# A decoder layer on one core: group loop rotated, blocks written in token layout, values and decay exponents in single-pass matmuls

## The chip, the cores and the metric

The kernel runs on 1 core of one Trainium2 chip. The metric is device time in microseconds (us), the median of three runs. The core has a matrix engine (PE), a vector engine (DVE), a scalar engine (ACT), GpSimd (POOL) and a DMA issuer (SP). Each engine executes its own instructions in the order in which they are written, and waits on semaphores that the others raise. Matrix results land in eight PSUM banks; everything else lives in SBUF. The weights come from HBM by DMA.

## The reference, cut to what matters

The layer takes x of 512 tokens by 1024 channels, in float32. One normalised input feeds an attention branch (16 heads in 4 groups, compressed, selected and window attention) and a state-space branch (32 heads in 4 groups); a gated MLP follows. With 512 tokens and 8 blocks of 64, top-8 selects every block, so the selected branch is causal attention over its own keys and values.

```python
h = rms_norm(x, norm1_w)
(q, k_c, v_c, k_s, v_s, k_w, v_w, g_nsa, z, xbc, dt_raw, gate_a, gate_b) = split_columns(h @ w_in, IN_SIZES)
# attention: for each head, branches c (31 compressed keys), s and w (512 keys each)
p_c = masked_softmax(s_c - slopes * d_c, vis_c) * any_visible
p_s = masked_softmax(q @ k_s.T - slopes * d, causal)
p_w = masked_softmax(q @ k_w.T - slopes * d, causal)
o   = gate0 * (p_c @ v_c) + gate1 * (p_s @ v_s) + gate2 * (p_w @ v_w)
# state space, chunks of 128 tokens
xbc = silu(causal_depthwise_conv(xbc, conv_w, conv_b))      # width 4
decay_mat = exp(segsum(dt * a))                             # 128 x 128 for each head and chunk
y_diag = (C @ B.T * decay_mat) @ (x * dt)
y = y_diag + exp(a_cum) * (C @ state) + d_skip * x
y = rms_norm_per_group(y * silu(z)) * norm_w
merged = sigmoid(gate_a) * (y_a @ w_proj_a) + sigmoid(gate_b) * (y_b @ w_proj_b)
x = x + merged @ w_out
x = x + (silu(gate) * val) @ w_down                         # after rms_norm, w_up and a width-3 conv
```

## The kernel before, in words

**Weight blocks.** All projections are cut into 175 units of 1024 x 128 weights. SP loads a unit into `wraw` (2 buffers). ACT copies it, rounded to the short format fp32r, into `whi` (`hi`, L847), DVE subtracts to get the rest `wlo` (`lo`, L1233); 3 slots. PE then makes three matmuls of 512 columns for each of 8 slices (`ktile`, L477): whi x h_hi, whi x h_lo, wlo x h_hi. The 24 matmuls of a block accumulate in one of two banks g. Weights are stationary and tokens stream, so a block comes out with channels on partitions. An fp32r matmul is one pass; an fp32 matmul is shown as two passes in the trace.

**Phases.** A start phase (9 blocks), the loop over 4 groups (14 blocks each), 12 blocks of gates, the two projections and their merge, the output projection, the MLP. `between` in `gemm` (L485) names what PE does ahead of the k-th of the 8 slices of a block: in this way all small work of the group loop stands between slices.

**The group loop** (L580 for PE, L957 for ACT, L1330 for DVE). Blocks 0 to 3 are x, 4 and 5 are B and C, 6 to 9 are z, 10 to 13 are the next group's queries, keys and values, kept in `chan`.

- *Start.* `to_tokens` (L588) transposes the four blocks of `chan`, ACT copies them to `tok`, DVE squares, sums (L1373, L1375) and takes a Newton root, scales six heads into `tokn` (L1382); `backs` (L595) transposes these back; ACT makes a full copy (`full`, L1003) and a rounded copy (L1005) of each, DVE subtracts (`head_lo`, L1388). `comp_scores` (L601) makes the compressed scores in 32 small matmuls.
- *Eight attention units* n = 0 to 7 (4 heads, 2 branches). `scores(n)` (L619) writes the causal scores in fp32r; `ttr` (L1404) adds the bias `hbias`, negates and reduces; `exps` (L1024) takes four exponentials; `scale` (L1445) multiplies by 1/sum and gate; `p_transposes` (L650) transposes ten 128 x 128 tiles through the banks t0 and t1 in four fills j = 0 to 3; ACT copies each fill to `pT` (L1045), which releases the bank (`t_rel`), and the weighted values (L675) follow behind the block of the unit, in fp32, with 64 rows of output. `conv` (L1339) makes the depthwise convolution on DVE: one tensor_scalar and three scalar_tensor_tensor.
- *State space.* x and z are transposed to tokens (`xz_transposes`, L685); `am` (L1480) builds a masked exponent matrix, `seg` (L696) multiplies it by a triangle in four fp32 matmuls of 128 columns for half a chunk; ACT exponentiates (`seg_e`, L1073); DVE multiplies by C B^T (L1523); PE applies the result (L735). Eight steps k, with state updates, `combine` (L1505) and a last root (L1549). Then y is scaled, transposed (L749) and spilled to HBM, to be read back for the projections.

## Time and profile before

| | before |
|---|---|
| median of 3 runs | 1397.42 us (1395.48 to 1399.1) |
| profiled execution | 1396.07 us, span 1394.3 us |
| mean granted TensorE clock | 0.991 |
| PE busy | 1336.0 us (96%) |
| PE weight loads busy | 1052.5 us (75%) |
| DVE busy | 822.7 us (59%) |
| ACT busy | 593.8 us (43%) |
| DMA | 116.27 MB, mean 83 GB/s |

A busy PE is not a PE at its peak: matmuls overlap, each shows some 0.4 us where the next starts after 0.23 us, so a matmul costs the distance between two starts. In the rows on DVE and ACT too, neighbouring instructions overlap by some 0.1 us, and the distance of the starts counts. `x8` in a timeline row stands for eight neighbouring instructions of one kind.

### The profile page before, as it was taken

What the parts mean: (1) busy time and instruction counts of PE and PEld (TensorE: products, weight loads), DVE (VectorE), ACT (ScalarE), POOL (GpSimd) and SP (SyncE); (2) the same over time, 40 slices, a digit from 0 to 9 for tenths busy, and PEclk for the clock granted to TensorE, in tenths of its full rate; (3) what the DMA queues carried; (4) which work ended last, traced back from release to release, by engine and by line L of the source; (5) the groups of instructions that cost most, each with busy time, mean ns of one, the idle gap of its engine ahead of it and who ended that gap; (6) DMA issues with size and microseconds to landing.
All of it is one profiled execution on the core that took longest, in us unless ns stands there. A gap on an engine that the chain in (4) does not pass through costs nothing.

```text
span 1394.3 us, 16620 instructions
## 1 busy us (share of the span) xinstructions
PE 1336.0 (96%) x6341; PEld 1052.5 (75%) x6341; DVE 822.7 (59%) x1546; ACT 593.8 (43%) x1050; POOL 4.1 (0%) x19
## 2 busy tenths in 40 slices
PE   3998999999998999989999999999999999999999
PEld 2787777777786776767777788887878888888887
DVE  3417855778567774777747353333368887886222
ACT  5524565455654546464564542222342223322120
POOL 1000000000000000000000000000000000000000
PEclk9999999999999999999999999999999999999999
DMA  8311212212112112121121833332423333333231
GB/s 251 76 47 31 61 53 53 77 31 67 48 38 77 46 54 68 32 76 46 54 68 35 280 105 96 91 91 91 167 62 105 91 91 91 97 100 106 102 118 68
DMA packets 185587, 116.27 MB, mean 83 GB/s; under 512 B 25917, under 2 KB 169637, under 8 KB 185509
## 3 DMA queue, kind: packets, MB, share of 16 engines
q1 hardware_dynamic: 182053, 108.92, 26.8%
q10 hardware_dynamic: 3456, 6.29, 1.2%
q8 instruction: 51, 0.84, 0.2%
q14 instruction: 27, 0.22, 0.0%
HBM read 106.80 MB, written 8.39 MB: 83 GB/s over the span
## 4 chain that ended last, share of the span: by engine, by line
PE 82%; DVE 9%; ACT 5%; issue 2%; SPq 1%; DMA 0%; ACTq 0%; DVEq 0%
PE g L481 18%; PE g L482 17%; PE g L483 17%; PE ob L675 5%; PE t L474 5%; PE s L631 3%; PE s L783 2%; PE s L785 1%; PE s L784 1%; PE s L610 1%; PE t L538 1%; DVE piece_e L1523 1%; PE g L783 1%; PE t L783 1%; PE t L785 1%
## 5 line engine op out<-in xcount | busy, mean ns | idle before, releaser
L1236 DVE TENSOR_TENSOR wlo<-wraw,whi 128x1024 fp32r<-128x1024 f32 x175 | 213.7, 1222 | 201.6 <-ACT whi L852 201.2
L852 ACT ACTIVATE whi<-wraw 128x1024 fp32r<-128x1024 f32 x175 | 184.8, 1057 | 261.9 <-DMA wraw<-in_ffn_w_up 140.4
L481 PE MATMUL g<-hT_hi,whi 128*128 128x512 f32 x616 | 264.5, 429 | 4.1 <-DVE hT_lo L1243 3.4
L482 PE MATMUL g<-hT_lo,whi 128*128 128x512 f32 x616 | 245.8, 399 | 0.0
L483 PE MATMUL g<-hT_hi,wlo 128*128 128x512 f32 x616 | 245.6, 399 | 0.0
L481 PE MATMUL g<-h2T_hi,whi 128*128 128x512 f32 x352 | 139.8, 397 | 0.0
L481 PEld LDWEIGHTS g<-hT_hi,whi 128*128 128x128 f32 x616 | 117.7, 191 | 29.2 <-issue 5.9
L482 PE MATMUL g<-h2T_lo,whi 128*128 128x512 f32 x352 | 139.5, 396 | 0.0
L483 PE MATMUL g<-h2T_hi,wlo 128*128 128x512 f32 x352 | 139.5, 396 | 0.0
L483 PEld LDWEIGHTS g<-hT_hi,wlo 128*128 128x128 f32 x616 | 117.1, 190 | 28.4
L482 PEld LDWEIGHTS g<-hT_lo,whi 128*128 128x128 f32 x616 | 118.0, 192 | 21.3 <-issue 1.9
L1045 ACT ACTIVATE piece_d<-t 128x512 f32<-128x512 f32 (+3 forms) x128 | 48.9, 434 | 121.3 <-PE t L474 120.7
L481 PEld LDWEIGHTS g<-h2T_hi,whi 128*128 128x128 f32 x352 | 66.3, 188 | 16.4 <-issue 0.2
L483 PEld LDWEIGHTS g<-h2T_hi,wlo 128*128 128x128 f32 x352 | 66.3, 188 | 16.2
L482 PEld LDWEIGHTS g<-h2T_lo,whi 128*128 128x128 f32 x352 | 66.3, 188 | 15.9
L483 PE MATMUL g<-yT_hi,wlo 128*128 128x512 f32 x192 | 76.1, 396 | 0.0
L481 PE MATMUL g<-yT_hi,whi 128*128 128x512 f32 x192 | 76.1, 396 | 0.0
L482 PE MATMUL g<-yT_lo,whi 128*128 128x512 f32 x192 | 76.1, 396 | 0.0
L675 PE MATMUL ob<-piece_d,tok 128*64 128x512 f32 (+3 forms) x256 | 75.8, 439 | 0.0
L1028 ACT ACTIVATE piece_b<-piece_a,negmx 128x512 f32<-128x512 f32 (+3 forms) x128 | 70.1, 554 | 1.7 <-DVE negmx L1411 1.6
L675 PEld LDWEIGHTS ob<-piece_d,tok 128*64 128x64 f32 x256 | 32.4, 136 | 46.4 <-issue 36.8
L1411 DVE CUSTOM_DVE_ANT_0 piece_a<-s,hbias 128x512 f32<-128x512 f32 (+3 forms) x128 | 55.1, 487 | 4.1 <-PE s L631 3.5
(293 smaller groups left out, 2069.9 us busy)
## 6 DMA issues: line engine op xcount, KB each, us to landing
wraw<-in_w_in SPq DMA_DIRECT2D x152, 256.0 KB, 3.2
wraw<-in_ffn_w_up SPq DMA_DIRECT2D x88, 256.0 KB, 3.2
wraw<-in_ffn_w_down SPq DMA_DIRECT2D x44, 256.0 KB, 3.2
wraw<-in_w_proj_b SPq DMA_DIRECT2D x32, 256.0 KB, 3.3
yT_lo<-spill SPq DMA_DIRECT2D x6, 1024.0 KB, 7.9
spill<-zchan ACTq DMA_DIRECT2D x16, 256.0 KB, 2.3
wraw<-in_w_proj_a SPq DMA_DIRECT2D x16, 256.0 KB, 3.3
wraw<-in_w_out SPq DMA_DIRECT2D x16, 256.0 KB, 3.5
```

The costliest lines, as they stand in the source:

```text
L474: last = nc.tensor.transpose(dst, src, ident[0:n, 0:n])
L481: nc.tensor.matmul(gb[par][:, :], w, hi, start=k == 0, stop=False)
L482: nc.tensor.matmul(gb[par][:, :], w, lo, start=False, stop=False)
L483: return nc.tensor.matmul(gb[par][:, :], wl, hi, start=False, stop=last)
L631: ins = nc.tensor.matmul(bk[:, o:o + w], qs[r][:, P * i:P * (i + 1)], k[:, 0:w], start=k is khh[br], stop=k is kll[br])
L675: ins = nc.tensor.matmul(orow[:, P * j:T], tok[:, 2 + br, j, DH:P], pT[:, offT[j]:offT[j] + w], start=br == 0 and j == 0, stop=False)
L783: nc.tensor.matmul(banks[i][:, :], hi, w[:, kk, :], start=start, stop=False)
L852: nc.scalar.activation(whi[u % SLOTS][:, :, :], wraw[u % 2][:, :, :], ACT.Copy).then_inc(w_hi, 1)
L1028: nc.scalar.activation(prob[n % 2][:, o:o + w], sneg[n % 2][:, o:o + w], ACT.Exp, scale=-1.0, bias=negmx[n % 2][:, i:i + 1], accum_out=rsu ...
L1045: nc.scalar.activation(pT[:, offT[j]:offT[j] + w], tb[par][:, 0:w], ACT.Copy).then_inc(t_rel, 1)
L1236: V.tensor_tensor(wlo[u % SLOTS][:, :, :], wraw[u % 2][:, :, :], whi[u % SLOTS][:, :, :].bitcast(F32), ALU.subtract).then_inc(w_lo, 1)
L1411: ins_ = V.tensor_tensor_reduce(sneg[n % 2][:, off[i]:off[i] + w], bk[:, o:o + w], hbias[r % 2][:, P * (3 - i):T], -1.0, 3e38, ALU.add, AL ...
```

## The change

**Order of blocks.** The loop is rotated. A group now begins with B and C, then come the four z blocks, the next group's four query, key and value blocks, and the next group's four x blocks. The first group's x blocks move ahead of the loop (13 blocks there, was 9); behind the last group 8 gate blocks are left (were 12), since the last group makes 8 gate blocks in place of the next group's. Four weight slots instead of three.

**Token layout.** z and query/key/value blocks are taken in pairs (16 pairs in all, `half_pair`): the tokens are stationary and two neighbouring weight slots stream, 48 matmuls of 256 columns for each half of the tokens. The result has tokens on partitions, so `to_tokens` and the z transposes go, and ACT's copies of them.

**Single passes.** The probabilities' transposes are rounded by ACT (`pT[0]`) and the rest is subtracted by DVE (`p_low`, `pT[1]`), which now is what releases the banks t0 and t1. Values are split into high and low, side by side in 128 stationary columns (`vst`); two fp32r matmuls replace an fp32 one. The two halves of the output are summed by `out_half` (ACT) and `out_fold` (DVE). The compressed part follows the same way, after every second unit. The weighted values of unit n stand inside the block of unit n+1.

**Decay exponents.** The strict triangle `gtr` is stationary, and the exponents times the other triangle stream in a high part (`am`, DVE) and a low part (`am_low`, ACT): two fp32r matmuls of 512 columns in place of four fp32 of 128.

**Moved between engines.** `full` is gone: `head_lo` reads the bank and releases it. The bias of a head is a copy on ACT (`head_bias`), with the mask in `negdist`. The first tap of the convolution is a second copy on ACT. The squares and root of the next group's heads (`qk_squares`, `qk_root`) stand in unit 7 and ahead of the state-space loop; the convolutions of the next group's x stand there, at the loop's end, and in the next start.

```diff
-SLOTS = 3
+SLOTS = 4
-PRE_BLOCKS = 9
+PRE_BLOCKS = 13
+EARLY_GATES = 8
+OB, OC, OZ, OQ, OX = 0, 1, 2, 6, 10
+PAIRS = {5, 8} | {U_GRP + GROUP_BLOCKS * g + o for g in range(G) for o in ((2, 4, 6, 8) if g < G - 1 else (2, 4))}
...
+            def half_pair(u, h, between=None):
...
+                for t in range(2):
+                    cols = slice(P * (2 * h + t), P * (2 * h + t + 1))
...
+                        w, wl = w_high[:, sl:sl + 2, k, :], w_low[:, sl:sl + 2, k, :]
+                        nc.tensor.matmul(out_, hT[0][:, k, cols], w, start=k == 0, stop=False)
+                        nc.tensor.matmul(out_, hT[0][:, k, cols], wl, start=False, stop=False)
+                        ins = nc.tensor.matmul(out_, hT[1][:, k, cols], w, start=False, stop=k == KD - 1)
...
+                def weighted_values(n):
...
+                    for j in range(NT):
+                        pe.wait_ge(t_rel, g * TG + (TP + K_UNIT[n] + j + 1))
+                        w = P * (NT - j)
+                        for part in pT:
+                            ins = nc.tensor.matmul(ob[:, P * j:T], vst[:, br, j, :, :].rearrange("p a d -> p (a d)"),
+                                                   part[:, offT[j]:offT[j] + w],
+                                                   start=br == 0 and j == 0 and part is pT[0], stop=False)
...
-                    for h in range(4):
-                        ins = nc.tensor.matmul((s1, s2)[k % 2][:, P * h:P * (h + 1)], amask[k % 2][:, h, :],
-                                               tri_le[:, :], start=True, stop=True)
+                    pe.wait_ge(am_lo, g * 8 + (k + 1))
+                    for a in range(2):
+                        ins = nc.tensor.matmul((s1, s2)[k % 2][:, :], gtr[:, :],
+                                               amask[k % 2][:, a, :, :].rearrange("p h n -> p (h n)"),
+                                               start=a == 0, stop=a == 1)
...
+            def evac_x(g, q):
...
+                nc.scalar.activation(xraw[q % 2][:, :], gb[u % 2][:, :], ACT.Copy)
...
+                nc.scalar.activation(conv_tile(q), gb[u % 2][:, :], ACT.Identity, scale=pcol[:, 0, col + 72 + CW:col + 73 + CW],
+                                     bias=pcol[:, 0, col + CB_:col + CB_ + 1]).then_inc(g_rel, 1)
+                hi(u + 3)
...
+                    for h in range(4):
+                        e = g * SE + 4 * (k % 2) + h
+                        ins_ = nc.scalar.activation(amask[k % 2][:, 1, h, :], tri_le[:, :], ACT.Copy,
+                                                    scale=adtr[:, 1, k // 2, e:e + 1].bitcast(F32))
...
+                nc.scalar.activation(zs[:, :, :], zs[:, :, :], ACT.Silu).then_inc(z_ready, 1)
+                out_half(3)
...
+                def p_low(n):
...
+                        V.tensor_tensor(pT[1][:, offT[j]:offT[j] + w], tb[(TP + K_UNIT[n] + j) % 2][:, 0:w],
+                                        pT[0][:, offT[j]:offT[j] + w].bitcast(F32), ALU.subtract).then_inc(t_rel, 1)
...
+                for n in range(8):
+                    scale(n)
+                    if n < 7:
+                        ttr(n + 1)
+                    if n in (2, 4, 6):
+                        out_fold(n // 2 - 1)
+                    lo(u0 + 4 + n)
+                    if n < 2:
+                        conv(g, 4 + n)
+                    if n == 0:
+                        comp_probs()
+                    if n == 2 and g < G - 1:
+                        key_consts(g + 1)
+                    if n == 7:
+                        am(0)
+                        am(1)
+                        if g < G - 1:
+                            dve.wait_ge(g_rel, u0 + OQ + 2)
+                            qk_squares(0)
+                            qk_squares(1)
+                    p_low(n)
...
+                if g < G - 1:
+                    conv(g + 1, 0)
+                    dve.wait_ge(g_rel, u0 + OQ + 4)
+                    qk_squares(2)
+                    qk_squares(3)
+                    qk_root()
```

Three places in the programs of the engines show how instructions move. First DVE in an attention unit of the first group, before; `ISA ... negmx` is the end of `ttr`, `wlo` the rest of a weight unit, `RECIPROCAL` the start of the next `scale`.

```order
L1411 ISA piece_a,negmx<-s,hbias 128x128
L1411 ISA negmx 128x1
L1236 TENSOR_TENSOR wlo<-wraw,whi 128x1024
L1345 TENSOR_SCALAR xc<-xraw,pcol 128x512
L1348 SCALAR_TENSOR_TENSOR xc<-xraw,pcol,xc 128x511
L1348 SCALAR_TENSOR_TENSOR xc<-xraw,pcol,xc 128x510
L1348 SCALAR_TENSOR_TENSOR xc<-xraw,pcol,xc 128x509
L1449 RECIPROCAL pscale<-rsum 128x4
```

The same place in the change, in unit 1:

```order
L1551 ISA piece_a,negmx<-s,hbias 128x128
L1551 ISA negmx 128x1
L1340 TENSOR_TENSOR w_low<-wraw,w_high 128x1024
L1385 SCALAR_TENSOR_TENSOR xbc<-xraw,pcol,xbc 128x511
L1385 SCALAR_TENSOR_TENSOR xbc<-xraw,pcol,xbc 128x510
L1385 SCALAR_TENSOR_TENSOR xbc<-xraw,pcol,xbc 128x509
L1608 TENSOR_TENSOR pT_lo<-t,pT_hi 128x512
L1608 TENSOR_TENSOR pT_lo<-t,pT_hi 128x384
L1608 TENSOR_TENSOR pT_lo<-t,pT_hi 128x256
L1608 TENSOR_TENSOR pT_lo<-t,pT_hi 128x128
L1616 TENSOR_TENSOR pcT_lo<-t,pcT_hi 128x256 x2
L1592 RECIPROCAL pscale<-rsum 128x4
```

The four `pT_lo` subtractions (and two `pcT_lo` here) stand between the convolution and the next unit's scaling; the first tap of the convolution is gone from DVE.

Second DVE ahead of the state-space loop of the first group: the product with the triangle (L1500), the weight unit, then the loop's first two operations (L1523, L1484) and a state copy, before:

```order
L1500 TENSOR_TENSOR piece_b<-s,tri_le 128x512
L1236 TENSOR_TENSOR wlo<-wraw,whi 128x1024
L1523 TENSOR_TENSOR piece_e<-piece_e,piece_b 128x512
L1484 TENSOR_TENSOR piece_e<-strict_gt,adt 128x512
L1531 COPY rstd<-piece_e 128x1
```

And in the change, where `xcx` is the next group's x, `sq` and `ss` the squares and sums of its keys, `newton` the root, and L1710 the loop's first operation:

```order
L1677 TENSOR_TENSOR piece_b<-s,tri_le 128x512
L1340 TENSOR_TENSOR w_low<-wraw,w_high 128x1024
L1385 SCALAR_TENSOR_TENSOR xcx<-xraw,pcol,xcx 128x511
L1385 SCALAR_TENSOR_TENSOR xcx<-xraw,pcol,xcx 128x510
L1385 SCALAR_TENSOR_TENSOR xcx<-xraw,pcol,xcx 128x509
L1394 TENSOR_TENSOR sq<-chan 128x4x64
L1396 TENSOR_REDUCE ss<-sq 128x4
L1394 TENSOR_TENSOR sq<-chan 128x4x64
L1396 TENSOR_REDUCE ss<-sq 128x4
L1317 TENSOR_SCALAR newton<-ss 128x32
...
L1329 SCALAR_TENSOR_TENSOR rstd_qk<-newton 128x32
L1710 TENSOR_TENSOR piece_e<-piece_e,piece_b 128x512
```

A convolution, two squares with their sums and a root now stand ahead of the loop's first product.

Third PE behind the last fill of a unit, before: `g` is the unit's block, `ob` the weighted values, `s` the next scores.

```order
L481 MATMUL g<-hT_hi,whi 128x512
L482 MATMUL g<-hT_lo,whi 128x512
L483 MATMUL g<-hT_hi,wlo 128x512
L675 MATMUL ob<-piece_d,tok 64x512
L675 MATMUL ob<-piece_d,tok 64x384
L675 MATMUL ob<-piece_d,tok 64x256
L675 MATMUL ob<-piece_d,tok 64x128
L631 MATMUL s<-khh,qs 128x512
L631 MATMUL s<-kll,qs 128x512
```

And in the change, behind the scores, in the block of the next unit:

```order
L549 MATMUL g<-w_low,hT_hi 128x256
L550 MATMUL g<-w_high,hT_lo 128x256
L689 MATMUL ob<-pT_hi,vst 128x512
L689 MATMUL ob<-pT_lo,vst 128x512
L689 MATMUL ob<-pT_hi,vst 128x384
L689 MATMUL ob<-pT_lo,vst 128x384
L689 MATMUL ob<-pT_hi,vst 128x256
L689 MATMUL ob<-pT_lo,vst 128x256
L689 MATMUL ob<-pT_hi,vst 128x128
L689 MATMUL ob<-pT_lo,vst 128x128
L696 MATMUL ob<-pcT_hi,vcg 128x512
L696 MATMUL ob<-pcT_lo,vcg 128x512
```

The weighted values moved past the next scores and into the next block, and the block's matmuls have 256 columns with the weights streaming.

## Rows read from the trace of the kernel before

**Rows 1.** The page, busy us, share of the span, instructions.

```profile
PE 1336.0 (96%) x6341; PEld 1052.5 (75%) x6341; DVE 822.7 (59%) x1546; ACT 593.8 (43%) x1050; POOL 4.1 (0%) x19
```

**Rows 2.** Windows of four stretches: start:end, length, busy us per engine, PEclk.

```profile
102.30:140.40 38.10, 32.74 (x170) 26.87 (x170) 28.07 (x74) 17.96 (x36) 0.00 (x0) 0.91 0.10 28
140.40:213.80 73.40, 73.40 (x350) 53.07 (x349) 51.16 (x132) 43.17 (x106) 0.00 (x0) 1.00 0.23 62
213.80:270.80 57.00, 52.85 (x307) 42.02 (x307) 38.56 (x73) 28.91 (x49) 0.00 (x0) 1.00 0.19 51
270.80:307.10 36.30, 33.06 (x172) 26.89 (x170) 25.18 (x61) 18.16 (x35) 0.00 (x0) 0.91 0.16 44
```

**Rows 3.** Timeline of PE, one attention unit: start, length, line, operation, count.

```profile
183.65 2.37 PE L675 MATMUL ob<-piece_d,tok 128*64 128x512 f32 x8
189.42 0.93 PE L474 MATMUL t<-ident,piece_b 128*128 128x128 f32 x7
194.10 2.37 PE L675 MATMUL ob<-piece_d,tok 128*64 128x512 f32 x8
```

**Rows 4.** Timeline of PE: neighbouring matmuls of 256 and of 512 columns.

```profile
186.87 0.28 PE L631 MATMUL s<-khh,qs 128*128 128x256 f32 x1
186.99 0.28 PE L631 MATMUL s<-kll,qs 128*128 128x256 f32 x1
188.26 0.39 PE L482 MATMUL g<-hT_lo,whi 128*128 128x512 f32 x1
188.49 0.40 PE L483 MATMUL g<-hT_hi,wlo 128*128 128x512 f32 x1
```

**Rows 5.** Timeline of PE: the compressed scores.

```profile
462.32 4.07 PE L610 MATMUL s<-kcg,qs 128*128 128x32 f32 x32 [0.43 <-issue]
```

**Rows 6.** Timeline of DVE, the same attention unit.

```profile
185.00 0.18 DVE L1449 RECIPROCAL pscale<-rsum 128x4 f32<-128x4 f32 x1 [3.08 <-ACT piece_b L1028]
186.61 0.75 DVE L1336 SCALAR_TENSOR_TENSOR hbias<-negdist,slopes,cmask 128x512 f32<-128x512 f32 x1
187.39 0.69 DVE L1411 CUSTOM_DVE_ANT_0 piece_a<-s,hbias 128x512 f32<-128x512 f32 x1
189.04 0.08 DVE L1411 DVE_READ_ACCUMULATOR2_ANT negmx<- 128x1 f32 x1
190.75 2.32 DVE L1348 SCALAR_TENSOR_TENSOR xc<-xraw,pcol,xc 128x511 f32<-128x511 f32 x3
```

**Rows 7.** Timeline of ACT: first of four exponentials, what follows them, a table load.

```profile
182.69 0.73 ACT L1028 ACTIVATE piece_b<-piece_a,negmx 128x512 f32<-128x512 f32 x1
184.87 0.58 ACT L992 ACTIVATE zchan<-g 128x512 f32<-128x512 f32 x1
...
221.08 1.28 ACT L1065 ACT_TABLE_LOAD   x1
```

**Rows 8.** Timeline of PE, state-space loop: first two steps, end of the loop.

```profile
239.23 1.00 PE L735 MATMUL ob<-piece_a,piece_e 128*128 128x64 f32 x8
240.06 1.11 PE L702 MATMUL s<-tri_le,piece_e 128*128 128x128 f32 x8
241.01 1.00 PE L735 MATMUL ob<-piece_a,piece_e 128*128 128x64 f32 x8
255.55 0.48 PE L481 MATMUL g<-hT_hi,whi 128*128 128x512 f32 x1
```

**Rows 9.** Timeline of DVE in that loop.

```profile
242.52 0.68 DVE L1484 TENSOR_TENSOR piece_e<-strict_gt,adt 128x512 f32<-128x512 f32 x1
243.12 0.68 DVE L1533 TENSOR_TENSOR piece_e<-piece_e,dec 128x512 f32<-128x512 f32 x1
243.84 0.69 DVE L1536 TENSOR_TENSOR piece_e<-piece_e 128x512 f32<-128x512 f32 x1
```

**Rows 10.** Timeline of DVE, from the last two squares to the token scaling.

```profile
277.12 0.42 DVE L1373 TENSOR_TENSOR sq<-tok 128x256 f32<-128x256 f32 x1
281.63 3.70 DVE L1382 TENSOR_TENSOR piece_e<-tok,rstd 128x512 f32<-128x512 f32 x6
```

More of the change, by code:

```diff
@@ L69, with slot_of, done_for_slot @@
 UNITS = U_DN + FB
-BX, BB, BC, BZ, BF = 0, 4, 5, 6, 10
+OB, OC, OZ, OQ, OX = 0, 1, 2, 6, 10
+X0_UNITS = (7, 10, 11, 12)
+PAIRS = {5, 8} | {U_GRP + GROUP_BLOCKS * g + o for g in range(G) for o in ((2, 4, 6, 8) if g < G - 1 else (2, 4))}
+def slot_of(u):
+    return (u if u < PRE_BLOCKS else u + 1) % SLOTS
+def done_for_slot(u):
+    before = [v for v in range(u) if slot_of(v) == slot_of(u)]
+    if not before:
+        return 0
+    return before[-1] + (2 if before[-1] in PAIRS else 1)
 class Count:
@@ L529, in _ @@
             transposes(9, 1, [(tb[1][:, P * i:P * (i + 1)], small[:, P * i:P * (i + 1)]) for i in range(NT)])
-            for b in range(2, 6):
-                pre_gemm(b)
+            for b in range(2, 5):
+                block_of(b)
+            half_pair(5, 0)
+            half_pair(6, 1)
             pe.wait_ge(pe_added, 4)
@@ L562, in second @@
                 ins.then_inc(t_fill, 1)
-            gemm(7, 1, [(7, 8)], hT, {0: hid_back, 4: second})
+            half_pair(8, 0, {0: hid_back, 4: second})
+            half_pair(9, 1)
             pe.wait_ge(adt_ready, 1)
@@ L694, in _ @@
+                    transposes(tau, par, [(tb[par][:, P * b:P * (b + 1)], xcx[:, b, P * c:P * (c + 1)])
+                                          for b in range(4)])
+                block_of(u0 + OX, {1: lambda: weighted_values(7), 4: lambda: xz_transposes(0), 5: lambda: xz_transposes(1),
                               6: lambda: xz_transposes(2), 7: lambda: xz_transposes(3)})
@@ L891, in _ @@
             hi(2)
+            hi(3)
             act.wait_ge(mm_done, 1)
@@ L998, in _, with evac_late, head_bias @@
+                def evac_late(q):
+                    if g < G - 1:
+                        evac_x(g + 1, q)
+                    else:
+                        evac_gate(u0 + OX + q, gate_tile(4 + q))
+                def head_bias(r):
+                    nc.scalar.activation(hbias[r % 2][:, :], negdist[:, :], ACT.Copy,
+                                         scale=slopes[:, g * R + r:g * R + r + 1]).then_inc(hb_ready, 1)
+                head_bias(0)
+                head_bias(1)
                 for e, (_, _, gain) in enumerate(HEADS):
@@ L1416, in _ @@
                 ttr(0)
-                head_lo(5)
+                for br in range(2):
+                    dve.wait_ge(v_hi, g * 2 + (br + 1))
+                    V.tensor_tensor(vst[:, br, :, 1, :], tokq[:, 2 + br, :, DH:P], vst[:, br, :, 0, :].bitcast(F32),
+                                    ALU.subtract).then_inc(v_lo, 1)
                 dve.wait_ge(s_fill, g * SG + 4)
```

647 lines of the change are left out of this document (360 added, 287 removed).

## The prediction, made before the changed kernel was run

> **What bounds the kernel now.** I read the page's busy line first: PE is busy 96% of the span, DVE 59% [rows 1]. The idle time of PE is small, so a PE stream that gets shorter can shorten the kernel, as long as nobody else comes late. Then the windows, cut where a group's parts meet [rows 2]: start (until the weighted values of unit 0) 36.3 us, the eight attention units 73.4, the state-space part 57.0. One such group is 166.7 us, and the change works inside the four groups; ahead of them and behind them it only moves blocks. The reader is to see that DVE is at 25.2 of 36.3, 51.2 of 73.4 and 38.6 of 57.0 us: about 52 us free in a group, but in places of its own.
>
> **What PE gains, for itself.** By distances of starts in the timelines:
> - Weighted values: 2.3 us for four fp32 matmuls (eight passes) [rows 3]. Now eight fp32r passes of the same widths; two neighbours of 256 columns stand 0.12 us apart, of 512 columns 0.23 [rows 4], so 2 x (0.23 + 0.18 + 0.12 + 0.08) = 1.25. Saves 1.05 x 8 = 8.4 us for a group. The compressed part: before 2 x 0.87 = 1.7, now 8 x 0.23 = 1.9.
> - Exponents: eight passes take 0.95 us [rows 8], now 2 x 0.23 = 0.47. Saves 0.48 x 8 = 3.8.
> - Transposes: 32 of 176 go. Seven stand in 0.68 us [rows 3], so 0.1 each: 3.2, with some 0.09 for each return to the block 3.9.
> - Pairs: 96 matmuls at 0.12 instead of 48 at 0.233: 11.5 for 11.2. Costs 0.3 x 4 = 1.3.
> In all 14.6 us for a group, 58 for four, if PE were alone.
>
> **What DVE gets.** Added for a group: `p_low` 8 x 1.75 (0.60, 0.48, 0.35 and 0.23 apart; an operation of 512 columns stands 0.60 us from its neighbour, 0.72 if the next reads its result [rows 9]) = 14, `out_fold` 2.4, the low values and compressed probabilities 1.4. Removed: first tap of six convolutions 3.3, bias 3.0. So 11.5 more, where PE has 14.6 less: 126 of some 152 us. That looks like enough room; the order decides. I followed both engines through a group. Durations: `scale` 1.6 (185.00 to 186.61), `ttr` 1.65 (187.39 to 189.04), a convolution's three taps 2.3 [rows 6], a weight unit 1.14, four exponentials 2.2 [rows 7], the smaller squares and root 4.5 (277.12 to 281.63) [rows 10].
>
> *Attention units.* The fills j = 2 and 3 need the banks of j = 0 and 1, which `p_low` now gives back, behind `ttr` and `lo`. Chain from `scale(n)`: 1.65 + 1.14 + 0.60 + 0.48 to the release, 0.6 to the last copy on ACT, 2.2 exponentials, 1.6 `scale`: 8.5 us. PE needs 5.76 + 1.4 (scores) + 1.1 (transposes) + 1.4 (values) = 9.7, or 10.1 with the compressed part; before 10.45 [rows 3]. So DVE has 1 to 1.5 us of slack, and what stands extra ahead of `p_low` comes through beyond it: unit 1 (a convolution) 1.1 us, unit 2 (fold, constants) 0.5, unit 7 (two `am`, two large squares, 4.1) 2.6. Sum of units 1 to 7: 12.0 + 10.6 + 9.7 + 10.1 + 9.7 + 10.1 + 10.8 = 73.0, for 73.4 to 72.9 before.
>
> *Start.* Two blocks 11.2, six `backs` 2.7, scores 1.4, waits for `head_lo` (now the release of its bank) 1.4: 16.7 us; compressed scores 4.5 (3.9 to 4.9 in the groups, one of them in [rows 5]): 21.2. Then DVE alone: the compressed softmax 2.1, `scale` 1.6, `ttr` 1.65, 1.6 until scores(1) are there, `lo` 1.14, convolution 2.3, compressed probabilities 2.1, first `p_low` 0.6: 34.4. PE stands at the third fill since 30.6. With the rest of the block 35.9, for 36.3. All of PE's gain here is waited away.
>
> *State space.* From the end of block 7: ACT has its copy, a weight unit, `am_low`, a table load of 1.28 [rows 7] and a silu of 1.9 before `out_half(3)`, so DVE gets `out_fold(3)` at 6.1 and works on without a gap: fold and constants 1.5, x times dt 4.9, triangle 0.7, weight unit 1.1, convolution 2.3, squares and root 4.5, first product 0.6: 21.7. PE is at the loop at 21.8. Before, DVE did two products, two masks, the state and the four skip products (6.4 us) while PE made its block; now they are all in the loop. From there to the eighth product DVE has fourteen operations at 0.605, states 2.9, skip 2.5, combines and off-diagonal parts 4.7, a weight unit 1.1 and 0.1: 19.8 us. PE alone would need 8 x 0.83 + 6 x 0.47 + 3 x 0.87 = 12.1; before, the loop took 16.3 (239.23 to 255.55) [rows 8]. Behind it two combines, an off-diagonal part, a convolution 2.3 and the root bring y at 51.9, PE waits 1.8 for it, and the group ends at 56.4, for 57.0.
>
> So a group with a successor goes from 166.7 to 165.3 us: 1.4 us less.
>
> **Ends.** The last group has no next x, squares or root: units 2.9 us less, state space some 6 less (DVE is 6.8 us ahead at the loop's start, and the loop comes to about 16). The first group: four blocks more ahead of it, four gates less behind it, which cancel (two pairs there cost 0.6), but its last x block ends right before the loop: copy 1.1, convolution 2.3, barrier and constants 3.2, scaling 0.7 before the first `backs`, where PE comes at 0.7. Its start gets from 38.7 us behind the last block to 42.5 plus 0.6: 4.4 more. The second half of the program keeps its cadence, 24 matmuls at 0.233 us or 5.6 us for a block; the eight gate blocks (45 us) must cover the reading back of y, six loads of 7.9 us that overlap: I count nothing, up to 3.
>
> **Sum** against the profiled execution (1396.07, span 1394.3): starts +4.4 - 3 x 0.4 = +3.2; units -3 x 0.3 - 2.9 = -3.8; state space -3 x 0.7 - 6.0 = -8.1. Together -8.7: 1387.4, and since the median of the runs is 1.35 above the profiled one, 1389.
>
> **Unknown prices.** A 256-column matmul in `half_pair` changes its stationary tile in two of three, in [rows 4] in every second. Lower bound 0.1165 (half of 0.233), upper 0.14 (the 32-column matmuls of [rows 5], each with its own load: 4.07/32 = 0.127, up to 0.145 elsewhere). I take 0.12, the nearest row. The lower end gives -0.3 x 16 = -5 us, the upper 96 x 0.02 x 16 = +31, less what DVE's waits cover, about +20. `am_low` (four copies of 128 columns, 0.2 each by the probabilities' smallest copy) lies on ACT beside DVE's longer steps: nothing; at twice that, 3 us more per group before the Xt copies. `p_low` reads PSUM as `ttr` does: 0.55 to 0.70 for 512 columns, +-4 us in all.
>
> The granted clock is 0.91 in both starts [rows 2]: after the compressed scores and the many transposes it lies at 1.2 of 2.4 GHz for some us. A PE that waits 4 us there may get one more such stretch: up to 1.7 us for a group, inside the range.
>
> The Trainium skill, "TensorE: Matmul & The Clock Gate", section on packing small matmuls ("What overlaps and what doesn't"), says that a weight load overlaps a running matmul only in another row group, and gives a load of 128 columns as 128/1.2 GHz, an estimate of 107 ns. By that a pair would cost 96 x (107 + 107) for 48 x (107 + 213) ns, 5 us more each. This case's trace does not agree: at 0.12 and 0.233 us [rows 4] the load is hidden nearly whole.
>
> **Rivals.**
> - *Weight loads come through in the pairs.* Mechanism: half the columns under each load, so the load of a new stationary tile is no longer hidden. For it: the 32-column matmuls cost 0.127 us or more though they stream next to nothing [rows 5]. Against: 0.12 in [rows 4]. At 0.14 it gives +20 over my sum: 1409, slower. It decides from 0.13 on.
> - *DVE's queue costs more than I followed*: each convolution, fold or square ahead of `p_low` or of the loop makes PE wait, PE's waits send the clock down, and ACT's `am_low` delays the exponentials. 3 to 6 us more in each group: 1400 to 1412, about 1405. For it: I followed one chain, real ones have more links. Against: prices come from the same engine and operations.
> - *PE's stream decides after all.* If the loop in the state-space part and the start run without DVE waits, the 58 us come, less 4 for the first group: 1343. Against: the 19.8 us of DVE in the loop. A half-way case, DVE's waits half of those counted (about 30 of 65 us), gives 1360.
>
> **Chances.** My case 0.45 (1378 to 1399), half-way or PE alone 0.2, weight loads 0.1, deeper DVE waits 0.25. Less than 0.3% (4.2 us) is what a measurement of this kernel can't tell from no change. From my case faster 0.32, same 0.12, slower 0.01; half-way all faster; deeper waits: 0.05 faster, 0.05 same, 0.15 slower; loads slower 0.1. Faster 0.57, same 0.17, slower 0.26. Range 1360 to 1412.
>
> **What would show it.** Per group: start 36, units 73, state space 56; PE waiting before L508 for DVE pT_lo in units 0, 1 and 7 (about 3.8, 1.1 and 2.6 us) and before the loop's products for DVE piece_e, some 8 us in each of the first three groups and little in the fourth; PE weight matmuls of 256 columns 0.12 us apart; DVE busy above 80% in the groups. I am wrong if PE's waits are under 10 us for a group (then it is much faster), if the pairs stand more than 0.13 apart, or if the gates wait for y.

## The result and the profile after

The change made the kernel slower: 1417.78 us (median of 4 runs, 1412.49 to 1419.86) against 1397.71 us for the kernel before (4 runs on the same chip), ratio 1.0139 with a 95% interval of 1.0109 to 1.017. The prediction was 1389, faster; 1418 lies outside its range of 1360 to 1412 as well. The profiled execution took 1419.86 us, span 1418.1 us, with a mean granted TensorE clock of 0.966 (before 0.991).

The page's busy line after the change, which answers to [rows 1]:

```profile
PE 1309.9 (92%) x6805; PEld 1099.4 (78%) x6805; DVE 871.0 (61%) x1670; ACT 636.5 (45%) x1175; POOL 3.7 (0%) x18
```

PE is busy 26 us less and is idle some 50 us more (108 for 58 of the span). DVE has 48 us more. The windows, cut as in [rows 2]: start (up to the end of unit 0's block), units 1 to 7, state space, for the groups 0 and 1; start:end, length, busy us of PE, PEld, DVE, ACT, POOL, then PEclk, DMA share and GB/s:

```profile
125.19:166.89 41.70, 30.36 (x179) 26.59 (x179) 32.59 (x76) 17.32 (x35) 0.00 (x0) 0.86 0.19 51
166.89:242.94 76.05, 69.66 (x521) 66.57 (x521) 51.35 (x144) 45.83 (x112) 0.00 (x0) 0.97 0.21 53
242.94:301.29 58.35, 52.21 (x243) 40.16 (x243) 49.17 (x96) 36.64 (x74) 0.00 (x0) 0.90 0.14 41
301.29:340.55 39.26, 31.22 (x179) 27.36 (x178) 25.92 (x54) 17.28 (x34) 0.00 (x0) 0.91 0.25 67
340.55:416.75 76.20, 69.84 (x521) 66.63 (x521) 51.36 (x144) 46.09 (x113) 0.00 (x0) 0.97 0.21 53
416.75:475.09 58.34, 52.34 (x244) 40.13 (x244) 49.16 (x96) 36.65 (x74) 0.00 (x0) 0.90 0.14 41
```

| us | before | predicted | after |
|---|---|---|---|
| first start | 38.1 | 43.1 | 41.7 |
| start of a later group | 36.3 | 35.9 | 39.3 |
| units | 73.4 | 73.0 | 76.2 |
| state space | 57.0 | 56.4 | 58.3 |
| group | 166.7 | 165.3 | 173.8 |

The first start is 1.4 us shorter than predicted; every other part of a group is 2 to 3.4 us longer. DVE is busy 51 us in the units, before and after. What is new is who waits. PE's waits, in us in total, times and longest:

```profile
PE t L508 <- DVE pT_lo L1608: 36.6, 18, 4.3
PE t L508 <- DMA drow<-in_ssm_a_log: 18.5, 1, 18.5
PE s L795 <- DVE piece_e L1710: 13.5, 12, 2.6
PE t L508 <- DVEq L1529: 9.0, 6, 2.0
PE t L508 <- DVE piece_e L1511: 7.0, 1, 7.0
PE s L658 <- DVE negmx L1551: 4.5, 3, 1.5
```

The first row is the new one (the second is a wait of the start phase that the kernel before has too): transposes that wait until DVE has subtracted and given back the bank. By place (PE's timeline, group 1: third fill of units 0, 1, 2, 6 and 7; the number in brackets is the wait ahead):

```profile
339.03 0.70 PE L508 MATMUL t<-ident,piece_b 128*128 128x128 f32 x3 [3.54 <-DVE pT_lo L1608]
350.05 0.70 PE L508 MATMUL t<-ident,piece_b 128*128 128x128 f32 x3 [0.46 <-DVE pT_lo L1608]
361.74 0.70 PE L508 MATMUL t<-ident,piece_b 128*128 128x128 f32 x3 [0.82 <-DVE pT_lo L1608]
402.50 0.70 PE L508 MATMUL t<-ident,piece_b 128*128 128x128 f32 x3 [1.94 <-DVE pT_lo L1608]
...
414.82 0.85 PE L508 MATMUL t<-ident,piece_b 128*128 128x128 f32 x3 [3.12 <-DVE pT_lo L1608]
```

The records also show stretches at 1.2 of 2.4 GHz: 97 us in all, 26 before. In group 1 they begin at 322.7 (6.8 us, in the compressed scores), 339.8 (3.4, right behind the wait of unit 0), 414.9 (3.4, behind that of unit 7), 445.6 (6.8, in the state-space loop) and 459.3 us (3.4). The pairs' pitch is 0.12 us at full clock and 0.21 at half (PE's timeline, in and behind unit 0):

```profile
332.05 0.28 PE L548 MATMUL g<-w_high,hT_hi 128*128 128x256 f32 x1
332.17 0.28 PE L549 MATMUL g<-w_low,hT_hi 128*128 128x256 f32 x1
...
340.13 0.42 PE L549 MATMUL g<-w_low,hT_hi 128*128 128x256 f32 x1
340.34 0.41 PE L550 MATMUL g<-w_high,hT_lo 128*128 128x256 f32 x1
```

### The profile page after: what moved, and what is told of

It is laid out like the page before. It is cut to its first block, busy times and chain, and to the rows that moved or that the text cites. A ratio compares the mean times of both kernels' runs of the same rounds, so it can differ in the third digit from the quotient of the medians.

```text
span 1418.1 us, 17819 instructions
## 1 busy us (share of the span) xinstructions
PE 1309.9 (92%) x6805; PEld 1099.4 (78%) x6805; DVE 871.0 (61%) x1670; ACT 636.5 (45%) x1175; POOL 3.7 (0%) x18
## 4 chain that ended last, share of the span: by engine, by line
PE 69%; DVE 17%; ACT 9%; issue 3%; SPq 1%; ACTq 0%; DMA 0%; DVEq 0%
PE g L515 13%; PE g L516 13%; PE g L517 13%; PE t L508 3%; PE g L548 3%; PE g L550 3%; PE g L549 3%; DVE w_low L1340 2%; PE s L674 2%; PE ob L689 2%; ACT w_high L912 2%; DVE xcx L1385 2%; PE s L845 1%; PE s L843 1%; PE s L844 1%
## 5 line engine op out<-in xcount | busy, mean ns | idle before, releaser
L912 ACT ACTIVATE w_high<-wraw 128x1024 fp32r<-128x1024 f32 x175 | 185.1, 1058 | 302.5 <-DMA wraw<-in_ffn_w_up 144.1
L1340 DVE TENSOR_TENSOR w_low<-wraw,w_high 128x1024 fp32r<-128x1024 f32 x175 | 213.2, 1220 | 116.3 <-ACT w_high L912 108.1
L515 PE MATMUL g<-hT_hi,w_high 128*128 128x512 f32 x360 | 157.0, 436 | 5.1 <-DVE hT_lo L1347 4.2
L548 PE MATMUL g<-w_high,hT_hi 128*128 128x256 f32 x512 | 156.3, 305 | 0.0
L549 PE MATMUL g<-w_low,hT_hi 128*128 128x256 f32 x512 | 147.8, 289 | 0.0
L550 PE MATMUL g<-w_high,hT_lo 128*128 128x256 f32 x512 | 147.7, 288 | 0.0
L516 PE MATMUL g<-hT_lo,w_high 128*128 128x512 f32 x360 | 147.3, 409 | 0.0
L517 PE MATMUL g<-hT_hi,w_low 128*128 128x512 f32 x360 | 147.0, 408 | 0.0
L515 PE MATMUL g<-h2T_hi,w_high 128*128 128x512 f32 x352 | 139.8, 397 | 0.0
L516 PE MATMUL g<-h2T_lo,w_high 128*128 128x512 f32 x352 | 139.5, 396 | 0.0
L515 PEld LDWEIGHTS g<-hT_hi,w_high 128*128 128x128 f32 x360 | 71.2, 198 | 21.9 <-issue 4.9
L508 PE MATMUL t<-ident,piece_b 128*128 128x128 f32 x320 | 49.8, 280 | 36.6 <-DVE pT_lo L1608 36.6
```

The lines of the kernel that those rows point to most:

```text
L508: last = nc.tensor.transpose(dst, src, ident[0:n, 0:n])
L515: nc.tensor.matmul(gb[par][:, :], w, hi, start=k == 0, stop=False)
L516: nc.tensor.matmul(gb[par][:, :], w, lo, start=False, stop=False)
L517: return nc.tensor.matmul(gb[par][:, :], wl, hi, start=False, stop=last)
L548: nc.tensor.matmul(out_, hT[0][:, k, cols], w, start=k == 0, stop=False)
L549: nc.tensor.matmul(out_, hT[0][:, k, cols], wl, start=False, stop=False)
```

## The experiments

Three theories stood: DVE's queue (what stands ahead of the operation that PE waits for); DVE's amount of work; the pairs. Beside them the question what the granted clock costs.

**Order in the units.**

```diff
+                    p_low(n, (0, 1))
+                    lo(u0 + 4 + n)
                     if n in (2, 4, 6):
                         out_fold(n // 2 - 1)
-                    lo(u0 + 4 + n)
+                    if n == 7:
+                        am(0)
+                        am(1)
+                    p_low(n, (2, 3))
                     if n < 2:
                         conv(g, 4 + n)
...
-                    if n == 7:
-                        am(0)
-                        am(1)
...
-                    p_low(n)
```

The first two subtractions of a unit, which free the banks for the third and fourth fill, now stand ahead of the weight unit. The weight unit, the fold and, in unit 7, the two `am` stand between them and the last two; the convolution, the constants and the squares come behind all four.

> Only the order on DVE in the attention units is changed: the first two subtractions of a unit (which give back the banks for the third and fourth fill) stand right behind the maxima of the next scores, the other two behind the weight unit, and fold, convolution, compressed probabilities, constants and squares behind them. Theory 1 (it is what is queued ahead of the subtraction that PE waits for, and each such wait also lowers the granted clock): the waits before the third fill in units 0 and 7 (4.3 and 3.1 us) go nearly whole, 5 to 7 us per group, with two of the half-clock stretches of 3.4 us: 1385 to 1397 us. Theory 2 (DVE simply has too much work in these stretches, whatever the order): the waits come back at the next scaling or at the weighted values, 1410 to 1420 us. Theory 3 (pairs or their weight loads are what costs): no change, 1418.

Measured: 1376.36 us (1372.01 to 1382.81), ratio 0.9849 (0.9818 to 0.9879). No instruction more or less, and it is 41 us faster than the changed kernel and faster than the kernel before. The first theory had the direction, but 1385 to 1397 was too little. Its waits:

```profile
PE s L795 <- DVE piece_e L1711: 13.6, 12, 2.6
PE t L508 <- DVE pT_lo L1608: 8.1, 12, 1.0
```

36.6 us became 8.1, and half-clock time 97 became 63. Its windows for group 1:

```profile
289.49:323.04 33.55, 30.41 (x179) 26.72 (x178) 21.94 (x45) 16.95 (x34) 0.00 (x0) 0.90 0.25 71
323.04:392.85 69.81, 67.48 (x522) 64.82 (x521) 50.87 (x147) 46.30 (x113) 0.00 (x0) 1.00 0.22 58
392.85:451.25 58.40, 52.09 (x245) 39.14 (x244) 53.81 (x105) 36.64 (x74) 0.00 (x0) 0.91 0.18 50
```

The units lose 6.4 us and the start (with unit 0's wait in it) 5.7; the state space stays. DVE does the same 51 us in the units, so its amount of work does not explain these 41 us.

**Low part left out, two ways.** PE multiplies the rounded part twice, so PE does the same work but both kernels compute something else than the layer; they only show times. The low part of the compressed probabilities is left out too. In the first kernel ACT's copy gives the bank back, in the second DVE does, with nothing to compute.

```diff
-   nc.scalar.activation(pT[0][...], tb[par][:, 0:w], ACT.Copy).then_inc(pT_hi, 1)
+   nc.scalar.activation(pT[0][...], tb[par][:, 0:w], ACT.Copy).then_inc(t_rel, 1)
```

> Leaves out the low part of the probabilities (both products of a pair read the rounded part, so PE does the same work): DVE makes no subtraction, and ACT's copy gives back the banks, as before the change. Theory 1 (bank release behind DVE's queue): the waits before the transposes (36.6 us in all for the subtractions) go, and with them 8 to 10 half-clock stretches of 3.4 us: 1360 to 1382 us. Theory 3 (pairs, weight loads, ACT's additions): stays above 1400 us.

```diff
-   V.tensor_tensor(pT[1][...], tb[...][:, 0:w], pT[0][...].bitcast(F32), ALU.subtract).then_inc(t_rel, 1)
+   dve.sem_inc(t_rel, 1)
```

> Leaves out the low part of the probabilities as well, but DVE still waits for ACT's copy and gives back the bank itself, at the same place of its queue: the 14 us of subtractions in a group are gone, the place in the queue stays. If the place in the queue is what costs: near the changed kernel in unit 0 (a wait of 3 to 4 us stays), total 1395 to 1410 us. If DVE's amount of work is what costs: near the kernel in which ACT gives the banks back, within 5 us of it.

Measured: 1368.67 us (ratio 0.9789, 0.9774 to 0.9804), inside the first theory's range, and 1388.69 us (0.9932, 0.9917 to 0.9947), outside both. At the changed kernel's place the subtractions themselves (14 us of DVE in a group) cost 29 us over the four groups, and the place in the queue another 20, with this wait left in the second kernel:

```profile
PE t L508 <- DVEq L1609: 17.5, 12, 2.6
```

Neither of the two answers that I had set against each other holds alone. In the new order of the units the kernel with the subtractions is 8 us above the one without them (1376 against 1369).

**Work put into the waits.** 14 matmuls ahead of unit 0's third fill, 12 in unit 7, 9 ahead of the loop, in each group.

```diff
+   for q in range(EXTRA[n]):
+       nc.tensor.matmul(bk[:, :], hT[0][:, q % KD, 0:P], hT[0][:, q % KD, :], start=True, stop=True)
```

> Work is added and nothing removed: in each group 35 matmuls of 512 columns whose results nobody reads, 14 ahead of the third fill of unit 0 (3.3 us in a wait of 4.3), 12 at the same place of unit 7 (2.8 in 3.1), 9 ahead of the first step of the state-space loop (2.1 in 2.6). That is 140 matmuls, 32.6 us of PE at full clock. Theory 1 (PE's waits lower the granted clock): the half-clock stretches behind these three places (3.4, 3.4 and 6.8 us in a group) go or shrink, half-clock time falls from 97 to 45 to 65 us, and the kernel gets faster although it does more: 1398 to 1412 us. Theory 2 (the clock falls for another reason, as for the short matmuls and transposes themselves, or the stretches cost nothing since DVE is late anyway): 1417 to 1425 us, with half-clock time unchanged or the time unchanged.

Measured: 1416.09 us (1414.77 to 1416.96), ratio 1.0131 (1.0114 to 1.0148), clock 0.983. Half-clock time fell from 97 to 50 us, as the first theory said; 47 us at half clock do what 23.5 us do at full clock. But the time did not come to 1398 to 1412: the median moved by 1.7 us, less than the spread of the changed kernel's own runs. 32.6 us of added work on PE cost nothing that can be told. Windows of group 1:

```profile
300.22:337.58 37.36, 33.85 (x194) 29.20 (x193) 26.46 (x55) 17.02 (x34) 0.00 (x0) 0.91 0.28 78
337.58:413.56 75.98, 71.97 (x535) 68.41 (x534) 51.41 (x146) 46.45 (x113) 0.00 (x0) 0.98 0.21 53
413.56:470.73 57.17, 49.33 (x253) 37.60 (x252) 48.67 (x98) 36.99 (x74) 0.00 (x0) 1.00 0.14 37
```

The stretch behind unit 0 was only moved (to 347.8 us). The wait of unit 1 grew from 0.46 to 1.67 us: a PE that runs faster there waits longer for the same DVE, and the units stay at 76. Start and state space got 1.9 and 1.2 us shorter. So work put into the waits does bring the clock back, and a group gets 3.3 us shorter by it (173.8 to 170.5); much of the rest is hidden behind DVE. This is a net figure and no upper bound: the places were not all well chosen. In the loop PE does not wait ahead of the first step but at the third, behind the four skip products (2.59 us), and the last group had no such wait in unit 7: between the y transposes of the third and the fourth group it takes 168.7 us where the changed kernel takes 166.1. And some 10 us at half clock are left in group 1.

**Exponents undone**, on top of the new order:

```diff
-   for a in range(2):
-       ins = nc.tensor.matmul((s1, s2)[k % 2][:, :], gtr[:, :], amask[k % 2][:, a, :, :]...)
+   for h in range(4):
+       ins = nc.tensor.matmul((s1, s2)[k % 2][:, P * h:P * (h + 1)], amask[k % 2][:, 0, h, :].bitcast(F32), tri_le[:, :], ...)
```

> On top of the new order of the subtractions (1376 us): one part of the change is undone, the decay exponents are again four fp32 matmuls of 128 columns with the masked exponents stationary, without a low part and without ACT's four copies for each half chunk. Theory 1 (the loop of the state-space part runs at DVE's pace, so PE's gain there buys nothing): within 4 us of 1376, the loop as long as before. Rival (PE's stream counts): 0.48 us x 8 x 4 = 15 us slower, 1391 us.

Measured: 1376.05 us (1370.35 to 1376.69), ratio 0.9836 (0.9815 to 0.9857); with the new order alone 1376.36. The 15 us that PE was to save by the single-pass exponents buy nothing, as the theory said: the loop runs at DVE's pace. Half-clock time was 43 us here against 63 with the same total.

**Pairs as ordinary blocks**, on top of the new order:

```diff
-                        half_pair(u, n % 2, between)
+                        block_of(u, between)
```

> On top of the new order of the subtractions (1376 us): the sixteen half pairs inside the loop that come after the start phase are computed as ordinary blocks (48 fewer matmuls of 256 columns for 24 of 512 in each, channel layout, so what is read as tokens is wrong). All copies, transposes and waits stay. It measures what the pairs cost PE. By the cadence in the trace (0.12 and 0.233 us): 0.3 us for each of 28 halves, 5 to 8 us faster, 1368 to 1372. Rival (weight loads show through in the pairs, or the pairs lower the clock): 15 us or more faster, below 1361.

Measured: 1377.57 us (1376.21 to 1378.26), ratio 0.9854 (0.9838 to 0.9871). This kernel leaves out the token layout, so what is read as tokens is wrong; it only shows a time. Not even the 5 to 8 us of the cadence come; PE's waits for DVE in starts, units and loop grew by 4.5 us instead (those for the heads' banks from 7.0 to 9.0). That fits a saving of PE of about this size, given back in waits. The rival of weight loads, 15 us or more, has fallen, and the distance of 0.12 us in the trace says the same.

**Heads early**, on top of the new order: queries, keys and values ahead of z.

```diff
-OB, OC, OZ, OQ, OX = 0, 1, 2, 6, 10
+OB, OC, OQ, OZ, OM, OX = 0, 1, 2, 6, 2, 10
...
+                    if n in (3, 5) and g < G - 1:
+                        dve.wait_ge(g_rel, u0 + OQ + n - 1)
+                        qk_squares(n - 3)
+                        qk_squares(n - 2)
+                    if n == 7 and g < G - 1:
+                        qk_root()
...
                     conv(g + 1, 0)
-                    dve.wait_ge(g_rel, u0 + OQ + 4)
-                    qk_squares(2)
-                    qk_squares(3)
-                    qk_root()
```

> On top of the new order of the subtractions (1376 us): the next group's four query, key and value blocks come ahead of the four z blocks in a group, so that their squares stand in units 3 and 5 and the root in unit 7, and no square or root stands ahead of the state-space loop. Theory 1 (DVE's queue ahead of the loop sets when PE starts it, 3.9 us of it are gone): the wait before the loop's first step (2.6 us) goes, with part of the half-clock stretch behind it; 2 to 4 us for each of three groups, 1362 to 1371 us. Rival (DVE's amount of work in the units is at its limit too): the waits come back in units 3, 5 and 7, 1374 to 1382 us.

Measured: 1371.63 us (1368.65 to 1372.78), ratio 0.981 (0.9796 to 0.9825): 4.7 us less, just outside the 1362 to 1371 expected. The state space fell from 57.2 or 58.4 to 55.4 us, and the longest wait in the loop from 2.6 to 1.3.

**The fourth head ahead of the convolution**, on top of the new order:

```diff
-                if g:
-                    conv(g, 2)
                 head_lo(3)
+                if g:
+                    conv(g, 2)
                 lo(u0 + 3)
```

> On top of the new order of the subtractions (1376 us): in the start of a group the fourth head's subtraction stands ahead of the weight unit's neighbour, the convolution, instead of behind it. Theory 1: the waits for the release of a bank by DVE in the starts (7.0 us in three groups) fall to 1 to 3 us, 1369 to 1374 us. Rival: the convolution is late for the block B instead and the wait only moves, 1375 to 1378 us.

Measured: 1385.41 us (1384.82 to 1387.98), ratio 0.9916 (0.9901 to 0.993), 9 us slower. Both theories missed it: PE's waits ahead of the compressed scores grew from 3.8 to 10.2 us. It led me to the chain that sets the start. In the changed kernel's trace, group 1, first on DVE:

```profile
310.53 2.31 DVE L1385 SCALAR_TENSOR_TENSOR xcx<-xraw,pcol,xcx 128x511 f32<-128x511 f32 x3
312.88 0.76 DVE L1526 SCALAR_TENSOR_TENSOR qs<-t,pcol,qs 64x512 fp32r<-64x512 f32 x1
315.19 1.22 DVE L1340 TENSOR_TENSOR w_low<-wraw,w_high 128x1024 fp32r<-128x1024 f32 x1 [1.55 <-ACT w_high L912]
316.44 1.66 DVE L1526 SCALAR_TENSOR_TENSOR qs<-t,pcol,qs 64x512 fp32r<-64x512 f32 x2
318.25 2.32 DVE L1385 SCALAR_TENSOR_TENSOR xcx<-xraw,pcol,xcx 128x511 f32<-128x511 f32 x3
320.60 0.69 DVE L1551 CUSTOM_DVE_ANT_0 piece_a<-s,hbias 128x512 f32<-128x512 f32 x1
```

and on ACT and PE at the same time:

```profile
312.94 0.60 ACT L976 ACTIVATE xraw<-g 128x512 f32<-128x512 f32 x1 [2.64 <-DVE xcx L1385]
313.43 0.77 ACT L978 ACTIVATE xbc<-g,pcol 128x512 f32<-128x512 f32 x1
314.09 1.06 ACT L912 ACTIVATE w_high<-wraw 128x1024 fp32r<-128x1024 f32 x1
```

```profile
321.45 5.70 PE L658 MATMUL s<-kcg,qs 128*128 128x32 f32 x32 [1.50 <-DVE negmx L1551]
```

ACT's copy of block B into `xraw` waits until the convolution has read that buffer; the next weight unit stands behind the copy on ACT, its rest behind that on DVE, then two heads, a second convolution, and only then the first maxima, for whose bank PE waits before the compressed scores. A later convolution pushes all of it: here ACT's copy of B waits 3.35 us for it.

**Convolutions early**: on top of the early heads, then on the changed kernel alone.

```diff
                 lo(u0 + 1)
+                if g:
+                    conv(g, 2)
...
-                if g:
-                    conv(g, 2)
                 head_lo(3)
+                if g:
+                    conv(g, 3)
                 lo(u0 + 3)
                 head_lo(4)
                 head_lo(5)
-                if g:
-                    conv(g, 3)
```

> On top of the early heads (1372 us): the third convolution of the next x stands behind the token scaling, where DVE waits 4 us for PE's first transposes back, and the fourth ahead of the weight unit in place of the end of the start. Putting the convolution later had cost 9 us, since ACT's copy of block B waits for it and the next weight unit stands behind that copy. Theory (this chain, convolution to ACT's copy to weight unit to the first maxima, sets the start of a group): the first maxima come some 2 us earlier, the wait before the compressed scores (4.5 us in three groups) goes, 1360 to 1368 us. Rival (the starts are set by the compressed softmax and the units behind it): 1370 to 1373 us.

> The changed kernel (1418 us) with the two convolutions of the start placed as in e9, and nothing else: the order in the attention units and the place of the heads stay as the change has them. Theory (the starts and the units cost independently of each other): the starts of the groups 1 to 3 fall from 40.5 us by 3 to 5 us each and the whole by 9 to 17 us, 1401 to 1409 us, with the waits of units 0 and 7 as before (4.3 and 3.1 us). Rival (an earlier start only makes PE wait longer at the third fill of unit 0, which DVE sets): the start's gain is given back there, 1414 to 1418 us.

Measured: 1353.85 us (1352.71 to 1357.27), ratio 0.969 (0.9676 to 0.9704), 18 us less than the early heads alone and more than expected (1360 to 1368); the start fell to 30.7 us:

```profile
290.01:320.67 30.66, 28.68 (x179) 25.31 (x178) 21.84 (x45) 16.93 (x34) 0.00 (x0) 0.94 0.30 78
```

On the changed kernel alone: 1401.66 us (1400.23 to 1406.27), ratio 1.0036 (1.0023 to 1.0049), 16 us less, inside what was expected. The start of group 1 is 34.3 us for 39.3, although the wait at unit 0's third fill is longer (4.33 us for 3.54); the units keep theirs:

```profile
302.69:337.01 34.32, 28.01 (x180) 24.75 (x178) 25.37 (x54) 17.61 (x36) 0.00 (x0) 0.97 0.29 77
337.01:412.74 75.73, 69.31 (x522) 66.23 (x522) 51.38 (x144) 45.76 (x111) 0.00 (x0) 0.97 0.21 53
```

ACT's copy of B and DVE's first maxima in this kernel (timelines of ACT and of DVE):

```profile
312.41 0.60 ACT L976 ACTIVATE xraw<-g 128x512 f32<-128x512 f32 x1 [0.71 <-PE g L517]
318.36 0.69 DVE L1551 CUSTOM_DVE_ANT_0 piece_a<-s,hbias 128x512 f32<-128x512 f32 x1 [0.26 <-DVE qs L1528]
```

The copy no longer waits for the convolution and comes 9.7 us into the start, where it was 11.6; the first maxima come at 15.7 for 19.3. So by the traces some 1.9 of the 3.6 us come through ACT and the rest by the order of heads and convolutions on DVE; the run moves both convolutions and does not take the two apart.

**Two that gave nothing.** The first group's constants behind the token scaling, and in addition the block behind the loop spread over the loop:

```diff
-                block_of(u0 + OX + 2)
+                for k in range(4):
+                    loop_step(k)
+                block_of(u0 + OX + 2, {k - 3: (lambda k=k: loop_step(k)) for k in range(4, 8)})
```

> The kernel e9 with the first group's constants (clearing two tiles, scaled distances, compressed values) moved from ahead of the first token scaling to behind it, where DVE waits for PE. The first group's PE wait of 7.0 us before the first transposes should fall to 3 to 4.5 us: 2 to 4 us less than e9. If the barrier and the copy of the last x block set that wait, less than 1 us.

> The kernel e10 with the block that follows the state-space loop spread over its last four steps (its slices fill the places where PE waits for DVE's products). PE has about 12 us of work of its own in a loop that DVE makes 20 us long. If PE's order is what costs there: 2 to 5 us less for each group, 1345 to 1358 us. If DVE's own chain to the end of the group (combines, root, y) sets it: the wait moves to the y transposes, within 4 us of e10; half-clock time falls in either case, since PE has no gaps in the loop.

Measured: 1355.1 us (ratio 0.9702, 0.9687 to 0.9717), no difference from 1353.85 that can be told, and not the 2 to 4 us less that were expected: the first group's wait fell from 7.0 to 3.9 us, but those for the heads' banks grew from 5.9 to 9.4. And 1359.63 us (0.9729, 0.9716 to 0.9743), 4.5 us slower. The state space took 55.8 us with the block in the loop, 54.3 or 55.4 without. PE's wait moved to the y transposes, as the second theory said (from 2.5 to 12.5 us in all, for ACT's scaling of y); the time is a little beyond its 4 us. The half-clock time did not fall, against both (mean clock 0.986 for 0.990).

The version with the order of the units, the heads early and the convolutions early is the best: 1353.85 us, 3.1% faster than the kernel before and 4.5% faster than the change as it was made. It contains every part of the change.

## Why the prediction was wrong

The case that came is the second rival, deeper DVE waits, and beyond its size of 1400 to 1412. What held, step by step:

- *PE's gain.* The pitch of a pair is 0.12 us, as taken. With every part of the change in it and DVE's order mended the kernel is at 1354, so much of PE's gain is there to be had.
- *DVE's durations and the loop.* The first product of group 1 stands at 438.60 us, 21.9 us behind the end of block 7 (21.7 predicted), and PE's loop lasts 20.3 us (19.8 predicted). The exponents undone change nothing, so the loop is bound as I said. But PE waits only 3.6 us in it where I had some 8: 6.8 us of it ran at half clock, and a slower PE fills its own waits.
- *Waits of units 0, 1, 2 and 7.* Unit 0 3.5 us, 4.3 in the first group (3.8 predicted), unit 7 3.1 (2.6), unit 1 0.5 (1.1), unit 2 0.8 (0.5).
- *Ends.* Behind the last group the program runs 602.7 us where it ran 625.2, the four gate blocks fewer; the gates do not wait for y.

What failed:

- **The start of a later group**, 35.9 predicted, 39.3 measured, 3.4 us in each of three groups. The failed step is the sum 11.2 + 2.7 + 1.4 + 1.4 = 16.7 us to the compressed scores. They began 20.2 us into the start (321.45 less 301.29), 3.5 us late. Its last term, 1.4 us of waits, was 4.5 in the trace: 1.98 and 1.02 us for the heads' banks, and 1.50 for the first maxima, a wait that I had not put into the sum at all. The compressed scores then took 1 us more than my 4.5, since they ran at half clock, and DVE's chain behind them 1.2 us less than mine. I followed PE and DVE; a link that makes DVE late goes through ACT (convolution, copy of B, weight unit). Moving two convolutions took 5 us off the start and 16 us off the whole, so it is shown that their place sets the start; the share of the link through ACT is read from the traces.
- **The units**, 73.0 predicted, 76.2 measured. I had no wait in unit 6, where there is one of 1.9 us, and from the weighted values of unit 6 to the end of block 7 it took 11.55 us, where I had 10.8. The wait of unit 6 comes through ACT as well. These are ACT's silus of the convolved x, B and C with their table load, its copy of half of the output, and DVE's fold, which waits for that copy and stands ahead of the weight unit and the subtractions:

```profile
395.13 1.28 ACT L1155 ACT_TABLE_LOAD   x1
396.43 1.91 ACT L1155 ACTIVATE xcx<-xcx 128x2048 f32<-128x2048 f32 x1
398.25 1.04 ACT L1156 ACTIVATE xbc<-xbc 128x1024 f32<-128x1024 f32 x1
399.31 0.60 ACT L1098 ACTIVATE hstage<-ob 64x512 f32<-64x512 f32 x1
399.94 0.68 DVE L1623 TENSOR_TENSOR hstage<-ob,hstage 64x512 f32<-64x512 f32 x1 [2.90 <-ACT hstage L1098]
```

With the first two subtractions ahead of the fold, the longest of these waits on PE is 1.0 us. I had written that the order decides, and it does: the order in the units, unit 0 included, was worth 41 us.

- **The state space**, 56.4 predicted, 58.3 measured. The step that failed is that y comes when DVE's root is done. The block behind the loop ran its first 3 us at half clock (0.43 us a matmul), ACT's copy of it stands ahead of ACT's share of the scaling of y, and that share began 1.2 us behind the root (DVE's last step of the root, then ACT):

```profile
467.72 0.16 DVE L1329 SCALAR_TENSOR_TENSOR rstd<-newton 128x4 f32<-128x4 f32 x1
466.98 0.60 ACT L976 ACTIVATE xraw<-g 128x512 f32<-128x512 f32 x1 [2.77 <-PE g L517]
469.09 1.32 ACT L1204 ACTIVATE zs<-zs,rstd 128x512 f32<-128x512 f32 x2
```

With the fills the clock is full there, ACT begins with the root, and the state space is 1.2 us shorter. The other 0.7 us stays open. In the last group 6.8 us from the last product on ran at half clock, ACT's share began 3.1 us behind the root, and the part from block 7 to the end of the group took about 55 us for 50.4 predicted.

- **The clock.** "Up to 1.7 us for a group, inside the range": half-clock time in a group went from 3 to 7 us to 24. With 14 of these 24 us gone, the fills took 3.3 us off a group (173.8 to 170.5), and 5.1 us off the whole profiled execution. So this term was too small, by at least 1.6 us in a group; what the rest of the half-clock time costs, no run shows. The order in the units took 41 us off with 34 us less at half clock, which can be 17 of them at most, so the clock is not the main cause. I expected more of it when I wrote the expectations.

Added up against the prediction: three later starts 10.1 us and the first one -1.4, the units of three groups 9.5 and of the last one 2.1, the state space of three groups 5.8 and of the last one 4.7. That is 30.8 of the 32.5 us between 1387.4 and 1419.86. How much of the units' 3.2 is the wait of unit 6 and how much unit 7's stays open: no run takes them apart.

Three readings in the prediction were off without deciding anything. The terms of the chain in a unit give 8.3 us, not 8.5. "DVE busy above 80% in the groups" contradicts its own sum, 126 us in 165; measured were 126 in 173.8, or 73%. And the rival of weight loads rested on 0.127 us or more for a matmul of 32 columns, read where part of the row ran at half clock. The first group has such a row at full clock, and there it is 3.72/32 = 0.116 us:

```profile
130.64 3.72 PE L610 MATMUL s<-kcg,qs 128*128 128x32 f32 x32 [0.44 <-issue]
```

## What to carry to other kernels

Where a change lets a queue-bound engine give back a buffer that a faster engine waits for, put that operation first in its unit and let everything that nobody waits for stand behind it; a busy share of 61% says nothing about this. Follow each chain through the third engine as well: here a copy on ACT waited for a convolution's buffer, and a fold on DVE for a copy on ACT; such links show as waits of ACT or DVE, not of PE. A gain on an engine counts only in the stretches where nobody makes it wait: undo the part in a version without the waits to see what it is worth.

## What the runs showed of the hardware

- The granted clock often fell right behind a wait: behind one of 3.5 us PE ran at 1.2 GHz for 3.4 us (matmuls of 256 columns 0.213 us apart for 0.12). Behind unit 6's wait of 1.94 us it did not fall. With matmuls put into the waits, 47 us of such time went away.
- A low mean clock need not cost its full price. 97 us at half clock and 50 us gave 1417.8 and 1416.1 us, though the second had 32.6 us more of PE work; much of what the clock gives back becomes a longer wait for DVE.
- Matmuls of 256 columns with a new stationary tile in two of three run at the pace of half a 512-column one (0.12 us for 0.233). The Trainium skill, "TensorE: Matmul & The Clock Gate", section on packing small matmuls ("What overlaps and what doesn't"), says that a weight load overlaps a running matmul only in another row group. The distance of 0.12 us does not agree, and neither do ordinary blocks in place of the pairs (1377.57 against 1376.36 us, with 4.5 us more of waits).
